# Eight z units of a hybrid layer by seven block products each

## The reference

```
h = rms_norm(x, norm1_g)
proj = h @ w_in                                # 1024 -> z, xbc, dt, q, k, v, g_ssd, g_att
y_ssd = ssd_branch(z, xbc, dt_raw, ...) @ w_ssd_out
y_att = swa_sink_branch(q, k, v, ...) @ w_attn_out
merged = sigmoid(g_ssd) * y_ssd + sigmoid(g_att) * y_att
x = x + merged @ w_out
h2 = rms_norm(x, norm2_g)
x = x + hier_moe(h2, ...)                      # 64 experts of 3 MiB, two for each token
...
# in ssd_branch, per chunk of 128 tokens and group of heads
yz = (y * silu(z)).reshape(b, s, G, SSD_D_INNER // G)      # z: 256 x 2048
return rms_norm(yz, ssd_norm_g...)
```

## Time and profile before

| | us |
|---|---|
| median of three runs | 1452.46 (1451.11 to 1452.58) |
| the profiled execution | 1453.14 |
| its span | 1451.5 |
| TensorE busy | 1375.7 (95%) |
| VectorE busy | 658.9 (45%) |
| ScalarE busy | 325.3 (22%) |
| GpSimd busy | 250.2 (17%) |
| mean granted clock of TensorE | 0.992 of full speed |

### The profile page before, as it was taken

How to read it: one execution, slowest core, us unless ns; L and a number is a source line. 1 busy time by engine, 2 the same in 40 slices (tenths; PEclk the granted TensorE clock), 3 DMA queues, 4 the chain that set the end, 5 groups by cost and what they waited for, 6 DMA issues and landing times.

```text
span 1451.5 us, 25501 instructions
## 1 busy us (share of the span) xinstructions
PE 1375.7 (95%) x10590; PEld 1143.2 (79%) x10590; DVE 658.9 (45%) x1482; ACT 325.3 (22%) x719; POOL 250.2 (17%) x202
## 2 busy tenths in 40 slices
PE   8999999999999999999999999998999997888776
PEld 6868889988899999988888999997666665555543
DVE  2526164212498895428853664554333232222211
ACT  1143401241111110121546631102111111111110
POOL 0000000000268887000001243830000000000000
PEclk9999999999999999999999999999999999999999
DMA  8343434224444444544333443389999999999997
GB/s 346 135 152 143 155 136 147 82 99 145 160 153 168 156 141 175 183 158 148 146 117 133 158 173 121 132 337 396 392 424 424 426 425 425 426 425 425 425 426 289
DMA packets 60258, 349.27 MB, mean 241 GB/s; under 512 B 12808, under 2 KB 13928, under 8 KB 21104
## 3 DMA queue, kind: packets, MB, share of 16 engines
q1 hardware_dynamic: 56832, 339.13, 59.5%
q10 hardware_dynamic: 2960, 6.40, 1.2%
q0 software_dynamic: 352, 2.11, 0.4%
HBM read 396.43 MB, written 1.51 MB: 274 GB/s over the span
## 4 chain that ended last, share of the span: by engine, by line
PE 85%; DMA 8%; DVE 3%; issue 2%; POOL 1%; SPq 1%; ACT 0%; ACTq 0%; DVEq 0%; POOLq 0%
PE bank L489 24%; PE bank L567 11%; PE bank L1313 9%; PE bank L503 7%; PE bank L976 4%; PE bank L1336 4%; PE bank L1347 4%; PE bank L1361 4%; DMA work<-w_gate_e_dram 4%; PE bank L1171 3%; PE bank L556 3%; DMA con_sb<-w_up_e_dram 2%; PE bank L701 1%; PE bank L657 1%; DMA hT<-w_up_e_dram 1%
## 5 line engine op out<-in xcount | busy, mean ns | idle before, releaser
L489 PE MATMUL bank<-hT,ring 128*128 128x256 f32 x1024 | 227.0, 380 | 0.2
L489 PEld LDWEIGHTS bank<-hT,ring 128*128 128x128 f32 x1024 | 192.4, 190 | 29.2 <-issue 4.0
L2154 DVE TENSOR_TENSOR xT<-xT,bank 128x512 f32<-128x512 f32 (+2 forms) x102 | 64.6, 640 | 231.8 <-PE bank L1336 187.9
L1313 PE MATMUL bank<-work 128*32 128x256 f32 x1056 | 134.1, 401 | 27.0 <-issue 12.1
L489 PE MATMUL bank<-work,ring 128*128 128x256 f32 x704 | 153.6, 379 | 0.0
L489 PEld LDWEIGHTS bank<-work,ring 128*128 128x128 f32 x704 | 133.5, 190 | 18.8 <-issue 1.0
L1313 PEld LDWEIGHTS bank<-work 128*32 128x32 f32 x1056 | 68.1, 115 | 56.9 <-issue 37.9
L1313 PE MATMUL bank<-ring,work 128*32 128x256 f32 x528 | 74.3, 406 | 10.7 <-issue 6.7
L1336 PEld LDWEIGHTS bank<-selw,work 128*128 128x128 f32 x320 | 57.4, 189 | 33.5 <-issue 25.4
L1336 PE MATMUL bank<-selw,work 128*128 128x256 f32 x320 | 80.0, 392 | 1.8 <-ACT work L2133 1.0
L1347 PEld LDWEIGHTS bank<-work 128*128 128x128 f32 x608 | 70.8, 192 | 7.8 <-issue 7.8
(11 more groups left out here) (437 smaller groups left out, 2619.0 us busy)
## 6 DMA issues: line engine op xcount, KB each, us to landing
work<-w_up_e_dram SPq DMA_DIRECT2D x35, 1024.0 KB, 26.3
work<-w_gate_e_dram SPq DMA_DIRECT2D x31, 1024.0 KB, 26.0
work<-w_down_e_dram SPq DMA_DIRECT2D x28, 1024.0 KB, 27.2
ring<-w_up_dram SPq DMA_DIRECT2D x22, 1024.0 KB, 4.8
ring<-w_down_e_dram SPq DMA_DIRECT2D x21, 1024.0 KB, 26.0
ring<-w_gates_dram SPq DMA_DIRECT2D x20, 1024.0 KB, 4.9
ring<-w_gate_e_dram SPq DMA_DIRECT2D x18, 1024.0 KB, 26.7
ring<-w_up_e_dram SPq DMA_DIRECT2D x15, 1024.0 KB, 26.6
```

The lines of the kernel that those rows point to most:

```text
L489: m = mm(b[:, j * SEQ:(j + 1) * SEQ], w[:, k, j * P:(j + 1) * P], tile(k), start=(k == 0), stop=(k == kt - 1))
L1313: m = mm(b[j * CAP:(j + 1) * CAP, 0:HIDDEN], xg[:, k, j * CAP:(j + 1) * CAP], w[:, k, :], start=(k == 0), stop=(k == KD - 1), tile_positio ...
L2154: return v.tensor_tensor(dst, a, b, ALU.add)
```

## The change

The eight z units are made by seven products too. For them the input block moves to the place of the standing operand (`by_token`), so that the result comes out by tokens as before. z and gates now form one list of 16 units, `in2`, with one set of input differences (in `spare[:, 0:2048]`, made once, in front of the wait for the attention's squares) and one place for the sums (the next 1536 columns of `spare`). The expert unit that lay in `spare[:, 0:SLOT]` is no longer issued ahead: the first five expert places change their order, and all expert units stand behind the ring. `seven` waits for the banks of one, b and a each just ahead of its first product. ScalarE's silu of a z unit now waits for VectorE's join of it. GpSimd no longer waits for the xs tiles before the gates' sums. At the end the four stores share one semaphore.

```diff
-        expert_slots = ([spare[:, 0:SLOT]] + [wide[:, n, :] for n in range(4, 8)]
+        expert_slots = ([wide[:, n, :] for n in range(4, 8)] + [spare[:, 0:SLOT]]
...
+        SEVEN_IN2 = [("w_z2", i) for i in range(8)] + [("w_gates2", i) for i in SEVEN_GATES2]
+        in2_mix = [block4(spare[:, 512 * n:512 * n + 512]) for n in range(4)]
+        in2_sums = [[block4(spare[:, SLOT + 512 * n:SLOT + 512 * n + 512]) for n in range(3)]]
...
                     for k in range(KH):
-                        m = mm(bank_[:, place * P:(place + 1) * P], w[:, k, :], b[:, k, :], start=(k == 0), stop=(k == KH - 1))
+                        still, moving = (b, w) if by_token else (w, b)
+                        m = mm(bank_[:, place * P:(place + 1) * P], still[:, k, :], moving[:, k, :],
+                               start=(k == 0), stop=(k == KH - 1))
...
+                place_free("one")
                 product_of(one, 0, w["A11"], x["B11"]).then_inc(product_ready, 1)
+                place_free("b")
                 product_of(b, 0, w["A12"], x["B21"])
                 pe.wait_ge(S(name + "_summed"), 4 * n + 2)
                 pe.wait_ge(S(name + "_mixed"), 2)
+                place_free("a")
...
             def fill_ssd(n):
                 if n < 2:
-                    to_tokens(("z", 2 * n + 2), "w_z2", hT)
-                    to_tokens(("z", 2 * n + 3), "w_z2", hT)
+                    seven_in2("w_z2", 2 * n + 2)
+                    seven_in2("w_z2", 2 * n + 3)
                 elif n < 4:
-                    to_tokens(("z", n + 4), "w_z2", hT)
+                    seven_in2("w_z2", n + 4)
...
-                if u == UNITS.index(("w_z2", 0, 2048)):
-                    name_, _, e_ = EXPERT_UNITS[0]
-                    sp.dma_start(place_of(0), A[name_][e_]).then_inc(place_landed(0)[0], 16)
...
-            pool.wait_ge(product_ready, made("xt", 0, 3))
-            weight_sums("gates2", "w_gates2", SEVEN_GATES2, gates2_sums)
+            weight_sums("in2", None, SEVEN_IN2, in2_sums)
...
             def z_gated(i):
-                act.wait_ge(product_ready, made("z", i))
...
+                key = ("in2", ("w_z2", i), "b")
+                act.wait_ge(S("in2_joined"), in2("w_z2", i) + 1)
...
                 if n < 4:
+                    z_units = (2 * n + 2, 2 * n + 3) if n < 2 else (n + 4,)
+                    for i in z_units:
+                        in2_one("w_z2", i)
                     silu_and_sine()
...
+            first_mixes("in2", hT, in2_mix)
+            last_mixes("in2", hT, in2_mix)
             dve.wait_ge(S("qk_squares"), nth("qk_squares"))
...
             mask_rows(0)
             mask_rows(1)
+            for i in range(2):
+                in2_upper("w_z2", i)
+                in2_joined("w_z2", i)
...
-                if n == 1:
-                    first_mixes("gates2", hT, gates2_mix)
-                if n == 3:
-                    dve.wait_ge(product_ready, made("z", 7))
-                    last_mixes("gates2", hT, gates2_mix)
+                if n < 4:
+                    for i in (2 * n + 2, 2 * n + 3) if n < 2 else (n + 4,):
+                        in2_upper("w_z2", i)
+                        in2_joined("w_z2", i)
```

More of the change, by code:

```diff
@@ L558, in half_unit, with seven @@
                 unit_read()
-            def seven(name, w_name, units, n, src, mix, sums):
+            def seven(name, w_name, units, n, src, mix, sums, by_token=False):
                 i, x = units[n], x_blocks(src)
@@ L573, in seven, with place_free @@
                 unit_product[-1] = number(name, i, "b")
-                for part in ("one", "a", "b"):
+                def place_free(part):
                     if used(name, i, part) > 1:
                         pe.wait_ge(bank_free(name, i, part), used(name, i, part) - 1)
+                place_free("one")
                 product_of(one, 0, w["A11"], x["B11"]).then_inc(product_ready, 1)
+                place_free("b")
                 product_of(b, 0, w["A12"], x["B21"])
@@ L594, in sevens, with seven_in2 @@
                     seven(name, w_name, units, n, src, mix, sums)
+            def seven_in2(w_name, i):
+                seven("in2", None, SEVEN_IN2, in2(w_name, i), hT, in2_mix, in2_sums, by_token=(w_name == "w_z2"))
             def first_unit(key, name, src):
@@ L1469, in _ @@
                 if u == 0:
-                    continue
-                elif u == 1:
-                    sp.wait_ge(product_ready, made("gates2", 0, "one"))
+                    sp.wait_ge(product_ready, made("in2", ("w_gates2", 0), "one"))
                     sp.wait_ge(S("yz"), TT * SSD_GROUPS)
-                elif u == 5:
-                    sp.wait_ge(S("gates2_joined"), 8)
+                elif u == 4:
+                    sp.wait_ge(S("in2_joined"), len(SEVEN_IN2))
                 elif u in (7, 8):
@@ L1506, in _ @@
                 sp.wait_ge(bank_free("scatter", GROUPS - 1, n), used("scatter", GROUPS - 1, n))
-                sp.dma_start(out[:, part, :], xT[:, part, :]).then_inc(S(f"stored{n}"), 16)
-            for n in range(4):
-                sp.wait_ge(S(f"stored{n}"), 16)
+                sp.dma_start(out[:, part, :], xT[:, part, :]).then_inc(S("stored"), 16)
+            sp.wait_ge(S("stored"), 4 * 16)
         @block.gpsimd
@@ L1522, in _, with weight_sums @@
             nc.gpsimd.memset(flat(T), 0.0).then_inc(S("inverse_cleared"), 1)
-            def weight_sums(name, w_name, units, sums):
-                for n, i in enumerate(units):
-                    u = UNITS.index((w_name, i, 2048))
+            def weight_sums(name, w_name, units, sums, first=0, last=None):
+                for n, i in list(enumerate(units))[first:last]:
+                    u = seven_unit(w_name, i)
                     w, depth = w_blocks(u), len(sums)
@@ L1644, in log_and_exp, with kept @@
                 nc.scalar.preload_act_table_set("natural_log_exp_and_others")
+            def kept(name, units, n, place):
+                act.wait_ge(product_ready, made(name, units[n], "one"))
+                if n >= len(place):
+                    act.wait_ge(S(name + "_joined"), n - len(place) + 1)
+                A_(place[n % len(place)][:, 0, :], at(name, units[n], "one")[:, 0:P], ACT.Copy).then_inc(bank_free(name, units[n], "one"), 1)
             act.dma_start(col_sb[:, 0:KD], A["cols"][:, 0:KD]).then_inc(S("first_cols_landed"), 16)
@@ L1723, in _, with attention @@
             log_and_exp()
-            def attention(name, heads, out_of, sink, sc, PT, fill):
+            def attention(name, heads, out_of, sink, sc, PT, fill, last=None):
                 def exps(h):
@@ L1765, in attention @@
                         weighed(h // 2 - 1)
+                if last is not None:
+                    last()
                 weighed(heads - 1 if whole else heads // 2 - 1)
@@ L1880, in _ @@
             root("norm_ffn")
[L1881 to L1886, removed]
             def silu_ff(i):
@@ L1985, in silu_xbc, with in2_one @@
                 A_(part, part, ACT.Silu).then_inc(S("xbc_ready"), 1)
+            def in2_one(w_name, i):
+                kept("in2", SEVEN_IN2, in2(w_name, i), gates2_kept)
             def fill_xbc(h):
+                if h == A_HEADS - 1:
+                    in2_one("w_z2", 0)
                 if h in (5, 11):
@@ L2081, in _ @@
             for i in range(4):
-                act.wait_ge(bank_free("gates2", i, "b"), used("gates2", i, "b"))
+                act.wait_ge(bank_free("in2", ("w_gates2", i), "b"), used("in2", ("w_gates2", i), "b"))
             A_(flat(gB), flat(gB), ACT.Sigmoid).then_inc(S("ssd_gate_ready"), 1)
@@ L2772, in _ @@
                 if c == 0:
-                    dve.wait_ge(bank_free("z", 2 * n), used("z", 2 * n))
-                    dve.wait_ge(bank_free("z", 2 * n + 1), used("z", 2 * n + 1))
+                    for i in (2 * n, 2 * n + 1):
+                        dve.wait_ge(bank_free("in2", ("w_z2", i), "b"), used("in2", ("w_z2", i), "b"))
                 mul(y, y, zs[:, c, part]).then_inc(S("yz"), 1)
@@ L2782, in _ @@
             for n in (4, 5):
[L2783 to L2784 removed]
+                in2_upper("w_gates2", SEVEN_GATES2[n])
+                in2_joined("w_gates2", SEVEN_GATES2[n])
             y_turned(7)
```

49 lines of the change are left out of this document (25 added, 24 removed).

## The result

The changed kernel takes 1459.67 us (median of five, 1458.26 to 1460.94). The kernel before, run beside it, takes 1452.04 us (five, 1451.11 to 1452.58). The ratio is 1.0052, with a 95% interval of 1.0041 to 1.0062: slower by 7.6 us, where 1.6 us faster was forecast. The profiled execution took 1458.26 us for a span of 1456.6, the shortest of the five. So the two traces differ by 5.1 us: the profiled execution lies 1.4 us under the median of its kernel, and that of before 1.1 us over its own.

What follows compares the result with a forecast made beforehand. TensorE was taken to bound everything ahead of the experts, DMA the last 450 us. TensorE's 3.1 us saved less 1.5 for the expert unit gave -1.6 us: 1450.8 us, range 1448.2 to 1454.4.

Steps and rivals of the forecast that it cites:

- 0.2 us of wait: Turn of y behind z unit 6: TensorE waits 0.2 us for y_norm(2), VectorE's join and multiplies being late.
- units 0 to 3, 6 and 7: GpSimd's sums in these z units cost 0, VectorE being idle or a gap lying ahead; units 4 and 5 cost 0.2 us.
- The spare time at the turn: At the turn of y, y_norm(2) had 1.43 us to spare, 0.66 of them gone with the shorter unit.
- Small edits: One semaphore for four stores, kept moved up in the file, ScalarE's 128-column copy of one in its waits: 0.
- The rule of port sharing: VectorE and GpSimd lock each other out for whole instructions: wait at the turn 1.3 us instead of 0.2, result 1451.9 us.
- The clock: First gate/up product, after TensorE's idle for guest weights growing to 4.7 us: no change taken, at worst 3.6 us lost.
- Rival 3: VectorE late at turns of y, waits of 2.2 and 1.4 us: slower, 1454.3 us; chance 0.13.
- z unit 2's wait: In the ssd loop, its b waits 1.7 us for a bank ScalarE frees in xs_kept; bounds 0 to 2.5.
- 0.2 us lost in a pair: GpSimd's sums beside a busy VectorE in z units 4 and 5 cost TensorE 0.2 us.
- the hole at 996 us: DMA gap until the next ring slot opens, 1.0 us lost; the expert unit moved behind the ring fills it.
- the extra expert unit: Expert transfer no longer loaded ahead: 2.5 us more in the full DMA regime, 1.5 left after the hole; between 0 and 2.5.
- the saving of 3.1 us: TensorE's sum before the experts: 5.2 - 1.7 - 0.2 - 0.2 = 3.1 us earlier, between 0.5 and 5.2.

Runs made afterwards that it cites:

- f5_before_sums_there: Kernel before, only gate unit 0's GpSimd sums made later, after the last xs tile of chunk 1: 1456.89 us against 1451.32 before.
- e1_sums_later: Changed kernel, GpSimd starting gate unit 0's sums only when VectorE has done y_norm(2): 1455.92 us against 1452.49 before.
- g2_masks_and_bank: Changed kernel, gate unit 0's sums after iteration 3's masks, y_norm(2) and ScalarE's reads moved earlier, including cb and chunk 0's xs tiles: 1451.37 us against 1452.32 before.
- e2_norm_first: Changed kernel, y_norm(2) moved ahead of xde and the masks in VectorE's iteration 3, sums unmoved: 1457.52 us against 1452.49 before.
- g1_sums_behind_masks: Changed kernel, gate unit 0's sums after iteration 3's masks, y_norm(2) and ScalarE's reads for gate unit 0's banks moved earlier: 1454.12 us against 1452.03 before.

## Why the prediction was wrong

**The step that failed** is in the part on VectorE: "0.2 us of wait" at the turn of y. It measured 4.98 us, and 4.2 us of clock behind it, where the sum had nothing. What showed in its place: GpSimd's four sums for gate unit 0 lay over xde, the masks and y_norm(2) of VectorE and made them 4.2 us longer. The prediction looked for contention behind the join of unit 6, at the d_skip multiply. That multiply took 0.69 us after the change; GpSimd's last sum for unit 6 ended just as it began. The same multiply one iteration earlier, behind unit 5, took 1.66 us, and lies in the chain. The prediction gave "units 0 to 3, 6 and 7" nothing because VectorE was idle or a gap lay ahead, and left out the unit behind unit 7. Its own sentence "in a pair the second unit starts its sums when the first has made its a" holds across the border from z to gates too: one place for sums ties gate unit 0 to z unit 7. The row of 778.02 was read for its duration and not for its hour. f5_before_sums_there shows that this move alone costs 5.6 us (2.9 to 6.7) and that it needs no seven-product z unit.

**The spare time at the turn** was also worked out too kindly: 1.43 us less 0.66 for one shorter unit. TensorE came 3.1 us earlier in all and VectorE 0.8, so 0.85 us of wait stood there ahead of the collision at the turn; e1_sums_later has 0.86 left. In the chain ahead of it stands ScalarE's copy of the first product, priced at 0 under "Small edits": the join of unit 6 waited 1.69 us for it and ended 3.5 us behind the unit, where the prediction had 1.2. What that copy costs alone no run shows.

**The rule of port sharing.** The rows showed 0.98 us lost by one multiply, and I put one such loss into the sum. After the change four operations lost 1.08, 2.13 for two and 1.00, and the four-column copy about 1 us; that is some 1.0 us for each, four fifths of a sum (1.27 us). The Trainium skill (SBUF — State Buffer, "Who interferes with whom") says that one of the two engines holds the shared ports for its whole instruction. The trace agrees in that the loss goes by instructions, not by bytes: 0.95 to 1.08 us for a copy of four columns and for xde alike. By the rule the prediction would have had 1.3 us of wait, at the wrong operations as well; what failed was which instructions meet, before how long they wait.

**The clock.** It was weighed at one place, the gap for the guest weights. The idle time there was forecast at 4.7 us and was 2.30, and the product took 3.67 us instead of 5.35, within the bounds given. That gain of 1.7 us is luck. In g2_masks_and_bank TensorE was idle for 2.33 us at the same place (1013.02, line 1330), and the product took 5.35. The length of the idle time alone does not decide whether the clock falls. At the new wait the clock was not weighed, since the wait was thought 0.2 us long.

**Rival 3** named the right engine and the right turn, with two waits of 2.2 and 1.4 us and 0.13 of chance. It had the join and the d_skip and z multiplies as the cause and no clock, so even it came out 5.4 us low.

**What was right.** Units of 6.25 us; TensorE 3.1 us ahead at the end of z unit 7; z unit 2's wait, 1.42 us with ScalarE's xs copy as releaser (1.7 forecast); 0.2 us lost in a pair; the hole at 996 us closed; the extra expert unit small (0.9 us measured alone, -0.9 to 1.7 by the interval, 1.5 forecast). But the saving of 3.1 us reached ssd_out in no run: the best, g2_masks_and_bank, has 1.2 us, and no faster time.

**What stays open.** Whether the expert unit takes the 1.2 us of g2_masks_and_bank: 1.5 as forecast would leave it 0.3 us slower than before, which its interval (1.6 us to either side) allows but does not show. Of the changed kernel one execution has a trace; a gap for the guest weights that costs 1.7 us more could account for others being slower, but this is not shown. A place for the sums in which gate unit 0's could again be made near 778 us, beside those of z unit 3, was not tried.

## What to carry to other kernels

When work moves to an engine that slows another beside it, as GpSimd does VectorE here, list the hours at which its instructions will run, not only their sum: a buffer that is now shared decides these hours. Ask for each instruction which of the other engine's it will lie over, and count about 1.0 us for each here, however small the victim (an addition with one input from a bank lost nothing). And price every new wait of TensorE twice, for itself and for the clock behind it. Moving the cause alone (e1_sums_later) left 2.5 of the 6.35 us in the stretch to ssd_out, moving the victim alone (e2_norm_first) 3.8, both together with ScalarE's order (g1_sums_behind_masks) 0.1. And compare stretches between two events of a trace, not hours: the first z unit of two executions began up to 2 us apart.

## What was not expected of the hardware

A copy of 128 x 4 values took 1.12 to 1.23 us beside GpSimd's sums instead of 0.17. Idle time of much the same length met both levels of the clock: 2.30 us in the changed kernel was followed by a product at full speed, 2.33 us in g2_masks_and_bank and 2.21 us in e1_sums_later by a granted clock of 0.50. The 4.98 us at turn_y(2) cost 4.0 to 4.2 us behind them, nearly as much as the wait; 21 unused matmuls in its place (4.85 us) kept the clock at 1.00.
